# A 1-core kernel of three blocks on Trainium2: the order of the first transfers, and expert groups of 96 slots

## What is computed

```python
mod = silu(c) @ w_ada + b_ada                     # 9 vectors of 1024
u = rmsnorm(x) * (1 + sc1) + sh1
h = x + 0.5 * gt1 * swiglu(u, w_ffn1_in, w_ffn1_out)
h = h + gt2 * token_mixing(rmsnorm(h) * (1 + sc2) + sh2, cos, sin, ...)   # cos, sin of positions
h = h + 0.5 * gt3 * swiglu(rmsnorm(h) * (1 + sc3) + sh3, w_ffn2_in, w_ffn2_out)
x = rmsnorm(h)
for l in range(2):
    x = layer_norm(ALPHA * x + mixers(x), ...)
    # a token goes to one group (best two scores summed), and to two experts in it
    x = layer_norm(ALPHA * x + moe(x), ...)
```

## Time and profile before

| | |
|---|---|
| Median of 3 runs | 1252.31 us (1252.28 to 1256.04) |
| Profiled execution: its own time | 1250.61 us |
| Its span | 1248.8 us |
| PE (TensorE) busy | 1143.2 us, 92% |
| DVE (VectorE) busy | 907.9 us, 73% |
| ACT busy | 646.0 us, 52% |
| POOL (GpSimd) busy | 85.6 us, 7% |
| DMA | 271.91 MB, mean 218 GB/s |

### The profile page before, as it was taken

The page is one execution under the profiler, slowest core; times in us unless marked ns, Lnnn a source line. Parts: engine busy times, 40 slices in busy tenths (PEclk is TensorE's granted clock), DMA queues, the critical chain, the costliest instruction groups (busy, mean ns, idle before and its releaser), DMA issues.

```text
span 1248.8 us, 24383 instructions
## 1 busy us (share of the span) xinstructions
PE 1143.2 (92%) x10443; PEld 896.7 (72%) x10443; DVE 907.9 (73%) x1107; ACT 646.0 (52%) x771; POOL 85.6 (7%) x104
## 2 busy tenths in 40 slices
PE   2899999899798899999899996999989999699995
PEld 2787777588686477777588765987858776598773
DVE  2789888477647776556567755999976775599995
ACT  2344444243444445444355435877756544587772
POOL 1601111160000100000000000000000000000000
PEclk9999999899899899999899996999989999799998
DMA  9899999344048757554463330799964334079980
GB/s 359 270 314 355 342 336 326 98 152 156 6 156 287 266 190 273 202 202 156 141 196 107 129 120 26 257 380 385 377 194 156 124 115 164 7 274 381 380 317 34
DMA packets 160492, 271.91 MB, mean 218 GB/s; under 512 B 9476, under 2 KB 99944, under 8 KB 160264
## 3 DMA queue, kind: packets, MB, share of 16 engines
q1 hardware_dynamic: 150312, 232.84, 53.8%
q0 software_dynamic: 7904, 29.25, 6.9%
q10 hardware_dynamic: 2176, 8.39, 1.8%
HBM read 269.41 MB, written 1.05 MB: 217 GB/s over the span
## 4 chain that ended last, share of the span: by engine, by line
PE 83%; DVE 8%; ACT 3%; issue 2%; POOL 1%; SPq 1%; DMA 1%; ACTq 0%; DVEq 0%; POOLq 0%
PE ps L699 68%; PE ps L1365 1%; DMA rbias<-in_router_bias_dram 1%; PE ps L1494 1%; DVE wlo L456 1%; SPq L552 1%; PE ps L805 1%; DVE bnst L2001 1%; PE ps L1084 1%; PE ps L1114 1%; PE ps L792 1%; PE ps L1124 1%; PE ps L1482 1%; PE ps L965 1%; PE ps L1345 1%
## 5 line engine op out<-in xcount | busy, mean ns | idle before, releaser
L456 DVE SCALAR_TENSOR_TENSOR wlo<-raw,whi 128x2048 f16<-128x2048 f32 (+3 forms) x228 | 488.0, 2173 | 46.7 <-ACT whi L431 45.7
L431 ACT ACTIVATE whi<-raw 128x2048 f16<-128x2048 f32 (+3 forms) x228 | 402.9, 1806 | 15.3 <-DMA raw<-in_w_ffn_in_dram 8.6
L699 PE MATMUL ps<-uhi,whi 128*128 128x256 f16 (+2 forms) x1208 | 326.8, 273 | 7.5 <-DVE ulo L2026 4.2
L699 PE MATMUL ps<-ulo,whi 128*128 128x256 f16 (+2 forms) x1208 | 326.5, 273 | 0.0
L699 PE MATMUL ps<-uhi,wlo 128*128 128x256 f16 (+2 forms) x1208 | 326.2, 273 | 0.0
L699 PE MATMUL ps<-whi,hreg 128*128 128x512 f16 x736 | 229.8, 381 | 0.0
L699 PE MATMUL ps<-area,whi 128*128 128x128 f16 (+2 forms) x2168 | 196.2, 222 | 0.0
L699 PE MATMUL ps<-area,wlo 128*128 128x128 f16 (+2 forms) x1084 | 190.0, 222 | 0.0
L699 PEld LDWEIGHTS ps<-area,whi 128*128 128x128 f16 (+2 forms) x2168 | 172.0, 99 | 10.4 <-issue 2.8
L699 PEld LDWEIGHTS ps<-uhi,whi 128*128 128x128 f16 (+1 forms) x1208 | 120.1, 99 | 31.8 <-issue 10.6
L699 PE MATMUL ps<-wlo,hreg 128*128 128x512 f16 x368 | 140.2, 381 | 0.0
(11 more groups left out here) (341 smaller groups left out, 1365.7 us busy)
## 6 DMA issues: line engine op xcount, KB each, us to landing
raw<-in_exp_w_gate_up_dram SPq DMA_DIRECT2D x64, 1024.0 KB, 7.5
raw<-in_w_ffn_in_dram SPq DMA_DIRECT2D x44, 1024.0 KB, 7.4
raw<-in_w_in_dram SPq DMA_DIRECT2D x34, 1024.0 KB, 6.0
raw<-in_exp_w_down_dram SPq DMA_DIRECT2D x32, 1024.0 KB, 8.1
area<-in_w_ada_dram POOLq DMA_DIRECT2D x48, 512.0 KB, 6.2
raw<-in_w_ffn_out_dram SPq DMA_DIRECT2D x22, 1024.0 KB, 7.8
raw<-in_w_out_dram SPq DMA_DIRECT2D x12, 1024.0 KB, 5.8
raw<-in_w_ada_dram ACTq DMA_DIRECT2D x4, 1024.0 KB, 11.6
```

What stands on the lines that cost most here:

```text
L431: act.activation(whi[:, u.slot, 0:n], raw[:, u.slot, 0:n], ACT.Copy, scale=SW)\
L456: dve.scalar_tensor_tensor(out=wlo[:, u.slot, 0:n], in0=raw[:, u.slot, 0:n], scalar=SW, in1=whi[:, u.slot, 0:n], op0=ALU.mult, op1=ALU.sub ...
L699: last = pe.matmul(o, st, mv, start=start and i == 0, stop=stop and i == 2, skip_group_check=True)
```

## The change

Four things change.

1. **First transfers.** The table `small` is split: its identity part goes with `c`, the rest is the twentieth of the small rows (`stack_in`). The input is issued by ACT after its first modulation block. Unit 0 is issued after the broadcasts, in `phase`.
2. **Angles.** GpSimd computes them after it has asked for late block 3, and ACT takes the Sin in chunk 9 of FFN 1. VectorE sums quarter 0 of the second modulation block ahead of the norm, the other two after it, and makes the low part of unit 0 last.
3. **Slots.** Groups have 96 slots: all matmuls, copies and activations over slots get 96 columns in place of 128 (per expert 192 in place of 256), the down product's stationary side has 96 columns, and the branch goes dense for a group of over 96 tokens.
4. **Ranks and gates.** The rank matmuls come before the last 8 of the 32 transposes, and `gates` before the gather copies of group 0.

The diff, cut to its core:

```diff
@@ SP @@
-            sp.dma_start(small[:, :], small_d).then_inc(const_in, 16)
-            for t in range(TT):
-                sp.dma_start(x[:, t, :], a["x"][0, t * P:(t + 1) * P, :]).then_inc(x_in, 16)
-            load(Unit(U_FFN1), ffn1.src("a", 0))
+            sp.dma_start(small[:, 0:P], small_d[:, 0:P]).then_inc(const_in, 16)
+            sp.dma_start(small[:, P:C_SMALL], small_d[:, P:C_SMALL]).then_inc(stack_in, 16)
...
             def phase(ph):
+                load(Unit(ph.u0), ph.src("a", 0))
                 load(Unit(ph.u0 + 1), ph.src("b", 0))
@@ GpSimd @@
-            pool.wait_ge(const_in, 32)
-            pool.wait_ge(rows_in, 48)
-            link(pool.tensor_copy(tr[0], posi))
...
             pool.wait_ge(ada_pe, 2)
+            def rope_tables():
+                pool.wait_ge(stack_in, 16 * 20)
+                pool.wait_ge(rows_in, 48)
...
             for b in range(ADA_FFN1):
                 ada_block(pool, b)
+                if b == 3:
+                    rope_tables()
@@ TensorE @@
-            pe.wait_ge(stack_in, 16 * 19)
+            pe.wait_ge(stack_in, 16 * 20)
...
+                token_major(0, 0)
+                token_major(0, 1)
+                token_major(1, 0)
                 pe.wait_ge(slots_in, 16)
                 pe.wait_ge(sel_made, l + 1)
...
                 pe.matmul(ps[:, 3, 72:76], ones, g1, start=False, stop=True).then_inc(rank_mm, 1)
+                token_major(1, 1)
...
-                                last = split_mm(ps[:, 4 + c % 2, col * P:(col + 1) * P], whi[:, u.slot, w], wlo[:, u.slot, w],
-                                                ugh[:, g, k, :], ugl[:, g, k, :], k == 0 and col == 0, k == KT - 1)
+                                last = split_mm(ps[:, 4 + c % 2, col * SLOTS:(col + 1) * SLOTS], whi[:, u.slot, w],
+                                                wlo[:, u.slot, w], ugh[:, g, k, 0:SLOTS], ugl[:, g, k, 0:SLOTS], k == 0 and col == 0, k == KT - 1)
...
-                with pe.If(count > P):
+                with pe.If(count > SLOTS):
@@ ACT @@
+                        act.wait_ge(ang_made, 1)
+                        act.activation(sinb[:, :], tr[0], ACT.Sin)
+                        act.activation(cosb[:, :], tr[1], ACT.Sin).then_inc(sin_made, 1)
...
             ada_first(act, 0)
+            for t in range(TT):
+                act.dma_start(x[:, t, :], a["x"][0, t * P:(t + 1) * P, :]).then_inc(x_in, 16)
...
+            act.wait_ge(stack_in, 16 * 20)
             rms(0)
             hi_part(act, Unit(0))
-            act.wait_ge(ang_made, 1)
-            act.activation(sinb[:, :], tr[0], ACT.Sin)
-            act.activation(cosb[:, :], tr[1], ACT.Sin).then_inc(sin_made, 1)
@@ VectorE @@
+            ada_first_sums(1, (0, HALF, D), range(2))
             rms_xn(0)
+            ada_first_sums(1, (0, HALF, D), range(2, 6))
             lo_part(dve, Unit(0))
-            ada_first_sums(1, (0, HALF, D))
...
+                gates()
                 gather(0)
-                gates()
                 emit(1)
...
-                        dve.scalar_tensor_tensor(out=e_h, in0=ps[:, 4 + c % 2, T:2 * T], scalar=SX / S, in1=e_act,
+                        dve.scalar_tensor_tensor(out=e_h, in0=ps[:, 4 + c % 2, 2 * SLOTS:4 * SLOTS], scalar=SX / S, in1=e_act,
```

More of the change, by code:

```diff
@@ L39 @@
 EXPERTS = 16
+SLOTS = 96
 HALF = 512
@@ L611, in _ @@
[L611 to L616, removed]
-            pool.wait_ge(ada_pe, 2)
+            pool.wait_ge(ada_pe, 2)
@@ L1340, in _, with token_major @@
                 last.then_inc(used, 1)
[L1342 to L1347, removed]
+                def token_major(t, i):
+                    for k in range(KT):
+                        last = pe.transpose(ps[:, 4 + 2 * i + t, :].bitcast(F16)[:, k * P:(k + 1) * P],
+                                            (uhi, ulo)[i][:, k, t * P:(t + 1) * P], ident16)
+                    last.then_inc(xt_mm, 1)
+                token_major(0, 0)
+                token_major(0, 1)
+                token_major(1, 0)
                 pe.wait_ge(slots_in, 16)
@@ L1362, in gather @@
                             for k in range(4 * half, 4 * half + 4):
-                                o = ps[:, 2 * i + half, (k % 4) * P:(k % 4 + 1) * P]
+                                o = ps[:, 2 * i + half, (k % 4) * SLOTS:(k % 4 + 1) * SLOTS]
                                 for t in range(TT):
-                                    last = pe.matmul(o, v[:, t, k * P:(k + 1) * P], p16[:, t, g * P:(g + 1) * P],
+                                    last = pe.matmul(o, v[:, t, k * P:(k + 1) * P], p16[:, t, g * SLOTS:(g + 1) * SLOTS],
                                                      start=t == 0, stop=t == 1)
@@ L1481, in slot_setup @@
                                 for j in range(2):
-                                    last = pe.matmul(ps[:, 6 + g % 2, i * P:(i + 1) * P],
+                                    last = pe.matmul(ps[:, 6 + g % 2, i * SLOTS:(i + 1) * SLOTS],
                                                      gate16[:, j, 16 * t + e:16 * t + e + 1].to_broadcast([P, P]),
-                                                     p16[:, t, g * P:(g + 1) * P], start=t == 0 and j == 0,
+                                                     p16[:, t, g * SLOTS:(g + 1) * SLOTS], start=t == 0 and j == 0,
                                                      stop=t == 1 and j == 1)
@@ L1493, in scatter @@
                             for v in (ysh, ysl):
-                                last = pe.matmul(ps[:, 2 * t + n, :], pT16[:, g, t * P:(t + 1) * P],
-                                                 v[g % 2][:, n * HALF:(n + 1) * HALF], start=False,
+                                last = pe.matmul(ps[:, 2 * t + n, :], pT16[0:SLOTS, g, t * P:(t + 1) * P],
+                                                 v[g % 2][0:SLOTS, n * HALF:(n + 1) * HALF], start=False,
                                                  stop=g == 3 and v is ysl, skip_group_check=True)
@@ L1888, in gather @@
                         act.wait_ge(ga_mm[l], 4 * g + 2 * half + 1)
-                        act.activation(ugh[:, g, 4 * half:4 * half + 4, :],
-                                       ps[:, half, :].rearrange("p (k n) -> p k n", k=4), ACT.Copy).then_inc(ga_hi[l], 1)
+                        act.activation(ugh[:, g, 4 * half:4 * half + 4, 0:SLOTS],
+                                       ps[:, half, 0:4 * SLOTS].rearrange("p (k n) -> p k n", k=4), ACT.Copy).then_inc(ga_hi[l], 1)
                 gather(0)
@@ L1919, in group_out @@
                         act.wait_ge(*((yn_mm, 4 * l + g + 1) if n == 0 else (used, at_down(l, 4 * g + 3).count(1))))
-                        act.activation(ysh[g % 2][:, n * HALF:(n + 1) * HALF], ps[:, 6 + n, :], ACT.Copy,
+                        act.activation(ysh[g % 2][0:SLOTS, n * HALF:(n + 1) * HALF], ps[0:SLOTS, 6 + n, :], ACT.Copy,
                                        scale=SX / S).then_inc(ys_hi[l], 1)
@@ L1944, in sparse @@
                             act.wait_ge(used, at_down(l, c - 3).count(1))
-                        act.activation(e_hi[:, c % 3, :], e_h, ACT.Copy).then_inc(e_hi_made, 1)
+                        act.activation(e_hi[:, c % 3, 0:2 * SLOTS], e_h, ACT.Copy).then_inc(e_hi_made, 1)
                         if c in (5, 9, 13):
@@ L1953, in _ @@
                 count = act.value_load(rr[0:1, 18, 0:1].bitcast(I32))
-                with act.If(count > P):
+                with act.If(count > SLOTS):
                     dense()
@@ L2049, in chunk_lo, with ada_first_sums @@
                 dve.tensor_tensor(hlo[:, par, :], h_f32, hhi[:, par, :], ALU.subtract).then_inc(h_lo, 1)
-            def ada_first_sums(b, cuts):
-                for k in range(6):
+            def ada_first_sums(b, cuts, ks=range(6)):
+                for k in ks:
                     if k % 2 == 0:
@@ L2607, in _ @@
                 count = dve.value_load(rr[0:1, 18, 0:1].bitcast(I32))
-                with dve.If(count > P):
+                with dve.If(count > SLOTS):
                     dense()
```

52 lines of the change are left out of this document (29 added, 23 removed).

## The result

The kernel after takes 1221.34 us, the median of four runs (1219.01 to 1222.81), against 1252.92 for the kernel before (1252.28 to 1256.04): 0.974 of its time, 95% interval 0.972 to 0.977. The forecast was 1214, with a range of 1207 to 1227. The profiled execution took 1219.01 us, span 1217.2, which is 31.6 less than the one before.

What follows compares the result with a forecast made beforehand. TensorE was taken as the bound, VectorE and DMA close behind. Front -12.5, FFN +0.5, layer 0 -12.5, layer 1 -15.2, transfers +1.5: -38.2 on the profiled 1250.61 gives 1212.4, as median 1214; range 1207 to 1227.

Steps and rivals of the forecast that it cites:

- rival 3: Experts: 96 columns take as long as 128, so only the front and 0.6 us a layer are won: 1239; chance 0.08.
- Rival 4: Experts: a group over 96 tokens sends a layer dense, 112 us more, 1337 with one such layer; chance 0.02.
- Front and FFN: Stretch before the experts: operand activations at 38.8 for 51.4, -12.5 us, and late blocks in the FFN cost +0.5.
- the first quarter's landing: Front: the second modulation weight block's first quarter lands at about 20.3 us, and TensorE's transposes start at 23.9.
- Rival 1: FFN 1: angles take 30 us, the fifth late block comes 16 us late, price 4 to 10 us: 1221; chance 0.13.
- the 0.5 us: FFN 1: cost of computing the angles there, delaying the fifth late block; 0 to 3 us, taken as +0.5.
- Layer 0: Layer 0's experts: VectorE becomes the bound and the stage ends at 909.5 for 922.1, -12.5 us before the transfers' cost.
- Start: Start of the expert stages: earlier gates and rank matmuls let the third low part end 4 us earlier.
- Layer 1: Layer 1's experts: the stage ends at 1217.4 for 1232.7, -15.2 us before the transfers' cost.
- The transfers: Experts' weight loads: faster demand eats some of the ring's lead, +1.5 us for both layers, bounds 0 and 8.
- rival 2: Experts: the DMA is the next bound, with waits in the ring of 3 to 5 us a layer: 1221; chance 0.13.
- the forecast's own signs of being wrong: TensorE idling in FFN 1, ACT waiting for weights in the experts, or operands coming after 43 us.

Runs made afterwards that it cites:

- slots experiment: The kernel after with 112 slots in place of 96: 1225.82 us, ratio 0.977.
- experiment on part 4: The kernel after with rank matmuls again behind all 32 transposes and gates behind group 0's gather copies: 1221.63 us, ratio 0.976.
- VectorE and the bytes relieved: The kernel after, VectorE's product with the gates left out in experts 1 to 15 and half of the down weights loaded: 1212.24 us, ratio 0.968.
- its repetition: The kernel after, unchanged, run again as base for the relief runs: 1220.14 us, ratio 0.973.
- units held: The kernel after, SP asking for weight units 0 and 1 only once the second modulation block's third and fourth quarters are in: 1220.62 us, ratio 0.973.
- VectorE relieved: The kernel after without VectorE's product with the gates in experts 1 to 15: 1222.64 us, ratio 0.975.
- third low part early: The kernel after, expert 0's third high and low part ahead of the wait for the gates' broadcasts: 1215.76 us, ratio 0.9705.

## Why the prediction was right, and where its steps were not

**The sign and the place held.** The forecast said that a shorter matmul would buy only what TensorE was slower than the next two, with VectorE as the next bound. The slots experiment and the windows show it. What the sentence left open is that the third bound, the transfers, stands level with the second. Price of a 96-column matmul: 45 forecast, 44.3 measured, so rival 3 is out. Rival 4 is out too: the experts' matmuls have 96 columns in both layers.

**Front and FFN, -12.0 forecast, -11.2 measured.** The step that was off is the first quarter's landing, 20.3 forecast and 23.4 measured. TensorE's transposes moved along, 26.5 for 23.9. In the profiled execution part of this came back by luck, with a direct product of 4.00 us for the forecast's 6.83, and the last quarter (33.4 for 31.2) decided in its place. The sum of the bytes was taken at 389 GB/s for the whole front; a window from 10 to 20 us has 324. And SP's queue took 114 GB/s (1.82 MB between 18 and 34 us) where the earlier trace rows gave 82, with two units under way and not one, and a third asked for at 18.2. Holding the units back brought VectorE's last sums 2.8 us earlier, so that is why the last quarter came late; it also showed that with the long product the last quarter is not what matters. Rival 1, TensorE idling in FFN 1, is out (149.23 us for the 1152 matmuls, 149.06 before); the size of the 0.5 us can't be checked. The prediction took the angles' removal as needed for the front; in the new order it is not (1223.36 with them in front).

**Layer 0, -11.8 forecast, -10.3 measured.** Three terms. *Start*: "the third low part ends 4 us earlier", 3.2 measured by the first low half (14.4 less the 11.2 of the front). Its reason failed: the 4.2 us of gates were worth nothing (experiment on part 4). The version without part 4 has 2.6 of the 3.2 already, so these come with the 96 slots, TensorE's shorter first expert among them (5.34 us for 5.67); the rest is no more than the two profiles of the kernel after differ by (24.3 and 25.0 us). *Chain*: from the first to the last low half 123.7 before, 118.3 after, 5.4 for the 6.3 forecast. *Tail*: from the last low half to the last scatter 1.8 us less, for the 2.3 forecast.

**Layer 1, -14.4 forecast, -10.0 measured: the largest miss.** *Start*: 4 us forecast, 1.0 measured. Besides the gates, TensorE stops for 1.01 us in the gather and its first expert takes 6.39 us, where layer 0's took 5.34: together 2.1 of the 2.2 us by which this start falls short of layer 0's. The granted clock was at 0.50 until past 1069 us, the lower of the two levels. Windows of the kernel after, columns as above:

```profile
1065.00:1067.00 2.00, 2.00 (x28) 2.00 (x27) 1.40 (x2) 2.00 (x2) 0.00 (x0) 0.50 0.04 12
1067.00:1069.00 2.00, 2.00 (x28) 2.00 (x27) 2.00 (x2) 0.88 (x1) 0.00 (x0) 0.50 0.01 4
1069.00:1072.00 3.00, 3.00 (x57) 3.00 (x56) 1.60 (x1) 0.01 (x1) 0.00 (x0) 0.77 0.62 203
```

In the kernel before it rose 4 us after the gather's start, and in layer 0 of the kernel after 5; here the gap came in between and it rose after 8 to 9. *Chain*: 121.4 before, 115.0 after, 6.4 for the 6.1 forecast. *Tail*: from the last low half to the last scatter 9.7 before and 7.1 after, 2.6 less, where 5.1 less were forecast: the forecast let TensorE have one down product left when VectorE was done, and it had 36 matmuls in a row, because its banks had waited for the group copies. Moving the copies gave 1.9 of it.

**The transfers, +1.5 forecast with bounds 0 and 8.** In the kernel after itself they cost next to nothing: halving the down weights leaves the chain at 117.4 and 114.6 us. So rival 2's 3 to 5 us a layer did not come, though its premise, transfers about as slow as VectorE, was nearer than its 0.13 said: the kernels with VectorE and the bytes relieved show the two level. One of the forecast's own signs of being wrong, ACT waiting for weights in the experts, did show, with 4.9 and 1.8 us; it cost VectorE 0.7 and 0.4.

**What was luck.** The two layers gave 20.3 us together, less than the 24 that their own bounds allowed. The total came out inside the range because the front lay well inside its bounds: the forecast's own bounds reach to 1222, with a front of only 9 us and late blocks that cost 3. The range went on to 1227 for rivals 1 and 2; both are priced at 1221, the measured time, and neither happened. What was mis-sized is the starts (by 0.8 and 3.0 us) and the tails (by 0.5 and 2.5), and nothing on the other side made up for it.

## What to carry to other kernels

When one engine is relieved, write down for every other resource the time per unit of work in the same stage, the transfers too: here TensorE's 7.2, VectorE's 7.8 and the transfers' 8.0 us an expert stood side by side, and relieving one of the last two alone shortens the chain by 0 to 1.1 us a layer, both together by 4. Moving an operation earlier only helps if what comes behind it on that engine is ready earlier too; look for the next wait before counting the move. And two chains that end within a microsecond are one bound: the edit that shortens both (the order of the transfers) is worth nearly all of it, the edit that removes one (the angles) at most that microsecond.

## What was not expected of the hardware

TensorE's direct product of 32 matmuls of one column took 6.83 us in the kernel before and in seven of the profiled kernels with the new front, but 3.75 to 4.05 in five others, the kernel after and its repetition among them, with no difference in the code up to there that would explain it. Around the end of the short ones the granted clock falls to 0.50, behind the long ones it reads 1.00. The operands came at 39.9 us in the mean of the five and at 40.5 in the mean of the seven.

In all twelve profiles with fewer slots (eleven with 96, one with 112), the gather of group 0 in layer 1 stops after 25 matmuls for 0.7 to 1.1 us, without a wait that the profile shows; the kernel before has 0.09 us there, and layer 0 of the kernel after nothing. What stops it was not settled. One transfer of instructions (0.02 MB) runs in each case about half a microsecond into the gather, 1.5 us ahead of the stop in the kernel after, but the kernel before and layer 0 have it too and don't stop.

At the end of layer 1 TensorE waits for the group copies, and what the clock does then differs from profile to profile. After waits of 3.5 and 4.0 us it fell to 0.50 (units held, VectorE relieved), after 3.2 and 3.1 it stayed at 1.00 (the kernel after, ranks and gates back), and of four waits of 2.7 us it fell after one (third low part early). A fall costs 1.7 to 2.8 us there.
